# VectorE's finish of an mLSTM item moved to the step of its scores, and the decay rows stacked on 36 partitions

## The reference

```python
b = jnp.cumsum(lfc, axis=-1)
logd = jnp.where(tril, b[..., :, None] - b[..., None, :] + igc[..., None, :], -jnp.inf)
m_t = jnp.maximum(b + m[..., None], jnp.max(logd, axis=-1))
dw = jnp.exp(logd - m_t[..., None])
s = jnp.einsum('bhtd,bhsd->bhts', qc, kc) * dw
num = jnp.einsum('bhts,bhse->bhte', s, vc) + ...
den = jnp.sum(s, axis=-1) + ...
h = num / jnp.maximum(jnp.abs(den), jnp.exp(-m_t))[..., None]
...
h = (h_f + rev(h_b)).transpose(0, 2, 1, 3)
```

## Time and profile before

| | |
|---|---|
| Median of 3 runs | 3072.72 us (3069.27 to 3076.68) |
| The profiled execution's own time | 3073.89 us |
| Its span | 3072.1 us |
| TensorE busy | 2847.2 us, 93% |
| VectorE, ScalarE busy | 1775.6 us, 58%; 1472.4 us, 48% |
| Mean granted clock of TensorE | 0.954 |
| mLSTM items of layer 0 | 1315 to 1508 us |
| mLSTM items of layer 1 | 2474 to 2592 us |

### The profile page before, as it was taken

How to read it: one execution, slowest core, us unless ns; L and a number is a source line. 1 busy time by engine, 2 the same in 40 slices (tenths; PEclk the granted TensorE clock), 3 DMA queues, 4 the chain that set the end, 5 groups by cost and what they waited for, 6 DMA issues and landing times.

```text
span 3072.1 us, 40636 instructions
## 1 busy us (share of the span) xinstructions
PE 2847.2 (93%) x14716; PEld 2246.3 (73%) x14716; DVE 1775.6 (58%) x2600; ACT 1472.4 (48%) x2316; POOL 39.8 (1%) x50
## 2 busy tenths in 40 slices
PE   7999999997999997988999998999998988889898
PEld 6667888665888886766776676777776666767897
DVE  4646675744888887322365544664664433555676
ACT  5536564643777765322334343552452423344654
POOL 0000000000000000000000100000000010000000
PEclk9999999998999999987999999899999888999999
DMA  6436785434999994311221212353452232333464
GB/s 196 131 103 200 246 273 175 136 104 138 301 328 313 323 318 139 103 41 35 69 86 55 73 61 70 110 171 110 149 165 64 76 89 76 101 93 109 133 183 144
DMA packets 352378, 444.81 MB, mean 145 GB/s; under 512 B 19552, under 2 KB 197856, under 8 KB 352208
## 3 DMA queue, kind: packets, MB, share of 16 engines
q1 hardware_dynamic: 349504, 434.40, 45.0%
q0 software_dynamic: 2144, 6.74, 0.7%
q10 hardware_dynamic: 560, 1.41, 0.1%
HBM read 441.43 MB, written 1.05 MB: 144 GB/s over the span
## 4 chain that ended last, share of the span: by engine, by line
PE 48%; DVE 5%; ACT 5%; issue 3%; PEldq 0%; ACTq 0%; DVEq 0%
PE ps L2101 12%; PE ps L2144 9%; PE ps L2114 6%; PE ps L2157 4%; PE ps L2148 4%; PE ps L2164 2%; ACT w_hi L947 1%; PE ps L2383 1%; PE ps L2087 1%; PE ps L2354 1%; PE ps L2366 1%; PE ps L2350 1%; DVE w_lo L1385 1%; DVE att L1861 1%; PE ps L2403 1%
## 5 line engine op out<-in xcount | busy, mean ns | idle before, releaser
L1385 DVE TENSOR_TENSOR w_lo<-raw,w_hi 128x1024 fp32r<-128x1024 f32 (+2 forms) x674 | 801.4, 1200 | 795.6 <-ACT w_hi L947 703.9
L947 ACT ACTIVATE w_hi<-raw 128x1024 fp32r<-128x1024 f32 (+2 forms) x674 | 688.1, 1034 | 343.4 <-PE ps L2114 151.3
L2144 PE MATMUL ps<-w_hi,h_hi 128*128 128x512 f32 (+1 forms) x992 | 416.9, 422 | 19.8 <-DVE h_lo L1785 14.1
L2144 PE MATMUL ps<-w_hi,h_lo 128*128 128x512 f32 (+1 forms) x992 | 390.8, 396 | 0.0
L2101 PE MATMUL ps<-h_hi,w_hi 128*128 128x256 f32 (+1 forms) x1056 | 314.7, 323 | 6.8 <-DVE arena L1413 3.7
L2101 PE MATMUL ps<-h_lo,w_hi 128*128 128x256 f32 (+1 forms) x1056 | 312.9, 321 | 0.6 <-DVE h_lo L2021 0.4
L2157 PE MATMUL ps<-w_lo,h_hi 128*128 128x512 f32 (+1 forms) x992 | 304.0, 391 | 0.0
L2144 PEld LDWEIGHTS ps<-w_hi,h_hi 128*128 128x128 f32 x992 | 196.1, 198 | 62.3 <-DVE h_lo L1785 16.4
L2101 PEld LDWEIGHTS ps<-h_hi,w_hi 128*128 128x128 f32 x1056 | 201.8, 191 | 34.8 <-ACT w_hi L947 7.9
L2144 PEld LDWEIGHTS ps<-w_hi,h_lo 128*128 128x128 f32 x992 | 195.3, 197 | 31.9 <-issue 1.8
L2157 PEld LDWEIGHTS ps<-w_lo,h_hi 128*128 128x128 f32 x992 | 188.2, 193 | 41.4
(11 more groups left out here) (279 smaller groups left out, 4317.9 us busy)
## 6 DMA issues: line engine op xcount, KB each, us to landing
raw<-in_w_in SPq DMA_DIRECT2D x196, 512.0 KB, 3.6
raw<-in_w_mod SPq DMA_DIRECT2D x96, 512.0 KB, 4.4
raw<-in_w_up SPq DMA_DIRECT2D x88, 512.0 KB, 4.1
raw<-in_w_gu_exp SPq DMA_DIRECT2D x64, 512.0 KB, 5.4
arena<-in_w_gu_exp SPq DMA_DIRECT2D x64, 512.0 KB, 5.1
arena<-in_w_gu_exp SPq DMA_DIRECT2D x64, 384.0 KB, 3.9
arena<-in_w_dn_exp SPq DMA_DIRECT2D x48, 512.0 KB, 6.6
raw<-in_w_gu_dense SPq DMA_DIRECT2D x44, 512.0 KB, 5.0
```

The source lines that it names most:

```text
L947: nc.scalar.activation(w_hi[:, half, 0:n], place[:, 0:n], ACT.Copy).then_inc(seg.sig.hi_ready, 1)
L1385: nc.vector.tensor_tensor(w_lo[:, half, 0:n], place[:, 0:n], w_hi[:, half, 0:n].bitcast(F32), ALU.subtract).then_inc(seg.sig.lo_ready, 1)
L2144: ins = mm(ps[:, 2 * h + p % 2, 0:width], x[:, k + c, p * P:(p + 1) * P], wh[:, c * width:(c + 1) * width], start=opens and c == 0 and x i ...
```

## The change

Three things change. The high and low decay rows come to lie in one tile `ml_both` of 36 partitions, the high part on partitions 0 to 3 and the low part on 32 to 35, with zeros between; the selector is copied to both places. One matmul then adds both parts, over up to 512 columns at once, and the mask follows as one matmul of 256 columns. So that the partitions between hold zeros, VectorE clears both tiles at step 0 of `ml_rows`, and ScalarE waits for that ahead of its two copies of the selector. And VectorE's `finish(i)` moves from step 2i + 3 to step 2i + 1, the step of `scores(i)`.

```diff
-        ml_hi = rounded("ml_hi", Y_AT, 2, 2 * T, parts=ML_H)
-        row_of_r = rounded("row_of_r", Y_AT + 4 * T, ML_H, P, parts=ML_H)
-        ml_lo = rounded("ml_lo", Y_LO, 2, 2 * T, parts=ML_H)
+        ML_LO, ML_K = 32, 32 + ML_H
+        ml_both = rounded("ml_both", Y_AT, 2, 2 * T, parts=ML_K)
+        row_of_r = rounded("row_of_r", Y_AT + 4 * T, ML_H, P, parts=ML_K)
...
+        rows_cleared = sem("rows_cleared")
...
                     softplus(st.rows[0:n, 0, :], st.arows[0:n, 0, :])
-                    nc.scalar.activation(row_of_r, row_of[0:ML_H, 0:ML_H, :], ACT.Copy)
+                    act.wait_ge(rows_cleared, st.at["rows_ready"] + 1)
+                    for at in (0, ML_LO):
+                        nc.scalar.activation(row_of_r[at:at + ML_H], row_of[0:ML_H, 0:ML_H, :], ACT.Copy)
...
                 n = 4 * ML_H
+                if j == 0:
+                    nc.vector.memset(ml_both.bitcast(F32), 0.0)
+                    nc.vector.memset(row_of_r.bitcast(F32), 0.0).then_inc(rows_cleared, 1)
...
                     av = st.arows[0:ML_H, :, :]
-                    settled(nc.vector.tensor_copy(ml_hi, av))
-                    nc.vector.tensor_tensor(ml_lo, av, ml_hi.bitcast(F32), ALU.subtract).then_inc(rows_ready, 1)
+                    hi = ml_both[0:ML_H]
+                    settled(nc.vector.tensor_copy(hi, av))
+                    nc.vector.tensor_tensor(ml_both[ML_LO:ML_K], av, hi.bitcast(F32), ALU.subtract).then_inc(rows_ready, 1)
...
                 if st.mode == "mlstm":
-                    if k % 2 and 1 <= k // 2 <= n:
-                        finish(k // 2 - 1)
+                    if k % 2 and k // 2 < n:
+                        finish(k // 2)
                     return
...
                             row = row_of_r[:, e["h"], :]
-                            for c in range(nk // T):
-                                keys = slice(e["k0"] + c * T, e["k0"] + (c + 1) * T)
-                                mm(dst[:, c * T:(c + 1) * T], row, ml_hi[:, d, keys], start=True, stop=False)
-                                mm(dst[:, c * T:(c + 1) * T], row, ml_lo[:, d, keys], start=False, stop=c > 0)
-                                if c == 0:
-                                    mm(dst[:, 0:T], ident_r[:, :], e["masks"][d], start=False, stop=True)
+                            mm(dst[:, 0:nk], row, ml_both[:, d, e["k0"]:e["k0"] + nk], start=True, stop=False)
+                            mm(dst[:, 0:T], ident_r[:, :], e["masks"][d], start=False, stop=True)
```

## The result

The kernel with the change takes 2958.84 us (median of four runs, 2955.43 to 2964.98); the kernel before, beside it on the same chip, 3073.84. The ratio is 0.9625, with a 95% interval of 0.9612 to 0.9639. So the sign and the two large causes stood, and the bound that the range rested on did not hold. A repeat of the same kernel (`e4_after_again`), beside a kernel before of 3075.89 us, gave 2964.77, a gain of 111 us.

The account below looks back on a forecast made before the run. TensorE was taken as the bound. 291.1 - (204.2 - 13.1) = 100.0 us at best, less 9 for lapses, 3 for short steps and 1 for additions: 87 us off 3073.9, so 2987 us; range 2969 to 3022.

Parts of the forecast that it names:

- the sign: Whole kernel: the change makes it faster, chance 0.95; slower 0.03, within 0.2% of no change 0.02.
- the bound that the range rested on: mLSTM stages: at most 100.0 us gained, 291.1 less (204.2 - 13.1), putting the kernel at 2973 at best.
- The bound and its reading: TensorE, busy 93% of the span, bounds the kernel; gains on another engine count only where TensorE waits for it.
- Part 1: TensorE's mLSTM scores: four short matmuls replace ten per 512-key item, two fewer per 256-key item; 13.1 us saved.
- Part 2: VectorE's `finish(i)` two steps earlier: TensorE's 43.4 us of waits at the scores go, but for 3 us.
- Part 3: TensorE's clock in the mLSTM stages: one in three of 16 512-key items still lapses, costing 9 us.
- The sum: Whole kernel: 100.0 us at best, less 9 for lapses, 3 for short steps, 1 for additions: 87 us gained, 2987.
- Part 4: Added VectorE memsets and second ScalarE copy per layer: cost nothing, at most 3.2 and 1.2 us if cover failed.
- The clock that does not recover: Rival, mLSTM stages: short matmuls with steps between shapes keep the clock low; gain 56 us, 3017; chance 0.2.
- the shorter wait: Rival: ScalarE starts exp late, 16 items each wait about 1 us, some lapsing; gain 68 us, 3005; chance 0.12.
- the slower outcome: Rival: VectorE stops for exp before low halves, TensorE loses 4.6 us at 24 items; 54 slower, 3127; chance 0.03.
- both edits did what they say: Rival denied here: scores still wait on something VectorE reaches no earlier; gain 0 to 15 us, 3065; chance 0.03.

Follow-up runs that it names:

- e1_finish_only: The kernel after with `finish` kept at its new place but the decay rows back on two 4-partition tiles with ten short matmuls: 2990.97 us, ratio 0.9731.
- e6_finish_128: The kernel with only `finish` moved and ten short matmuls kept, both row tiles and the selector made 128 partitions tall with zeros: 2958.13 us, ratio 0.9612.

## Why the prediction was right or wrong

**The bound and its reading: right.** TensorE set the end, and what it stopped waiting for came out at the end of the kernel. No transfer and no other engine took the wait's place.

**Part 1, 13.1 us for fewer matmuls: right in itself, a little low.** The chain gives 1.48 us for the four, where 1.56 stood. Between `e1_finish_only` and after the stages differ by 20.3 us; less the 6.9 of lapses that is 13.4. The stages hold 22 of the 24 items, for which the prediction's prices give 12.2. The step into q.k, which it put at some 0.04 us, is worth 0.19 (0.86 in place of 1.05). So a gain beyond 13.1, which it excluded, was there. The bound above it, 9.6 us given back for 36 partitions, was not needed: 256 more columns of the stacked matmul cost 0.11 us. What the term left out is that the ten matmuls also carry lapses, below.

**Part 2, the stall gone and 3 us left: right, the rest smaller.** 0.8 us of waits are left. `finish` ends 4.6 us after q.k, and low halves are covered. The first step of it does most: in the stages, the run with a one-step move differs from after only in layer 1. The item intervals, forecast at 9 us with 512 keys in layer 0 and 8 in layer 1, were 8.8 and 9.2: the 8 did not fit the prediction's own work for layer 1, 69.7 us less 4.9 over seven intervals.

**Part 3, 9 us for lapses that stay: the step that failed.** "The item at 1315.3 lapsed with no gap ahead of it, so the rows decide" took the rate at which items with ten short matmuls and six steps between shapes lapse, and charged it to items with four of each. The rate itself was fair for the old scores: the kernel that had only its stalls removed kept 6.9 us of lapses, one of them behind that same item. With four steps and four short matmuls (after), or ten and no step (`e6_finish_128`), no lapse was left in the stages: 0 us in place of 9. Parts 1 and 3 were costed as independent, and they were not. The Trainium skill (TensorE: Matmul & The Clock Gate, Why this matters for your kernels), by which no lapse would be left once the stalls were gone, comes out right for the stages of after, but `e1_finish_only` speaks against it as the whole rule: its first stretch has no gap (TensorE busy 80.10 of 80.10 us), and lapsed.

**The sum.** The stages were forecast at 191.1 us of work, 9 of lapses, 3 of waits and 1 of additions, 204.1 in all, and took 188.4. Of the 15.7 us between, 9 are the lapses, 2.2 the waits and 1 the additions, which were hidden as argued; the other 3.5 are what is left over. Part 1 gave 0.3 of it (13.4 for the 13.1 charged); the rest lies in the work taken as busy time times a mean clock of two digits, an estimate that no run tests by itself. So the best gain of 100.0 us, 291.1 less the 191.1 of that estimate, was no bound: the stages alone gave 102.7.

**Part 4, additions at nothing: right.** The memsets take 0.91 and 0.48 us and end at 1245.4, ahead of a low half and of the idle time of the earlier trace rows, which is still there, 9.43 us long, up to 1257.3.

**Outside the stages: put at nothing in the forecast, and missed.** The range allowed "a few us below the bound, for stages beside these that gain from an earlier start". It was 10 us in the stretch between the layers, by a clock of 0.98 in place of 0.97, and 3.6 at the last item of layer 1, which the sum charged for its matmuls but not for its lapse; 4 us came back ahead of the first item. Together, 15.7 in the stages and about 12 outside by medians (115 - 102.7) make the 28 us by which the forecast missed. Part 3 alone is a third of that: without its 9 us the forecast would have been 2978, still 19 above the result. That the time fell below 2969 is due to this term and to the bound that was none, and the cause of its largest piece, the 10 us, is open.

**The rivals.** The clock that does not recover fell with 1.00 in all three stages; the shorter wait with 0.8 us; the slower outcome with an unchanged 2.8 us of waits for low halves, against 110 us at stake; and both edits did what they say. The rule named with the first rival, that of the Trainium skill (TensorE: Matmul & The Clock Gate, A second HAM failure mode: psum-queue depth-cycling), by which small idles between groups of matmuls suffice, would fit the pair `e1_finish_only` and `e6_finish_128` if the steps between shapes were such idles, which no run shows; six steps and ten matmuls went with 6.9 us, four steps and four matmuls with nothing.

## What to carry to other kernels

When a short step of the bounding engine waits for a slow one, look first at where the slow engine's work stands in its own queue: here 85 of 111 us came from moving work that was not late by its amount, but by its place. Short matmuls with few partitions between full ones are paid for at the step between shapes, so zeros up to the common shape can be faster than a smaller matmul; in the one pair tried here the clock stayed up with them too. And a forecast that adds up parts should ask whether one part removes the cause of the cost that another part charges; its best case is a bound only if the work itself is measured, not worked out from a mean clock.

## What the runs showed of the hardware that was not expected

A step from one matmul shape to another costs in the stream what the columns do not explain: 0.31 to 0.32 us for a matmul of 256 columns behind such a step against 0.12 without, and ten matmuls without any take 0.12 each, 1.18 us in all against 2.22.

```profile
1320.30 0.12 PE ps L2356
1320.41 0.12 PE ps L2357
1320.53 0.12 PE ps L2359
1320.65 0.12 PE ps L2356
```

(The first four of the ten in `e6_finish_128`, in its chain of waits; L2359 is the mask.) The clock fell to 1.2 GHz with TensorE never idle by the profile: in `e1_finish_only` the first stretch is busy 80.10 of 80.10 us at a clock of 0.96, and the same ten matmuls without steps between shapes ran at 1.00.

The granted clock outside the changed stages did not stay the same either. The stretch between the layers, the same but for one item's matmuls and the additions, ran in 963.3 to 974.0 us, so that a difference of 5 to 10 us between two versions of this kernel can come from stages that neither touches, and only windows cut at the same instructions tell.
